# Six mix operations behind the scale, the low parts of the mixes on GpSimd, and two more hidden tiles split early

## The chip, the cores and the metric

The kernel runs on one NeuronCore of a Trainium2 chip. The metric is the device time of one execution in microseconds. Before the change it is 3221.83 us, the median of three runs (3221.02 to 3222.63). Five engines run queues of their own and wait for each other through semaphores: TensorE (PE) multiplies, VectorE (DVE) and ScalarE (ACT) work element by element, GpSimd (POOL) does the same more slowly, and SyncE (SP) issues the loads of weights.

## The reference

Two blocks stand one behind the other over 512 positions of width 1024, all in float32. The first has two kinds of attention, a cross attention and a gated MLP; the second has two layers. Each of these two layers holds two SwiGLU feed-forwards, four in all, and the change is in these:

```python
def swiglu(x, w13, w2):
    gate, up = jnp.split(x @ w13, 2, axis=-1)
    return (jax.nn.silu(gate) * up) @ w2

h = h + 0.5 * rms_norm_2(swiglu(rms_norm_2(h, g[0]), ffn_w13[i, 0], ffn_w2[i, 0]), g[1])
```

The inner width is 2816, that is 22 tiles of 128.

## The kernel before

A float32 value is multiplied as a high part and a low part. ACT makes the high part (a cast, `split_hi`, L329 for weights), DVE subtracts it from the value to make the low part (`split_lo`, L345), and PE does three products: high by high, low by high, high by low (L528). Weights come in chunks of 128 x 2048 float32 (1 MB), in two slots.

Each feed-forward has three stretches. The texts call the four feed-forwards FF1 to FF4; they start their mixes at about 903, 1554, 1978 and 2810 us.

1. The first four units of the up projection (gate and value of one hidden tile each), in `linear` with `paired="filled"`. The norm is deferred: PE multiplies the unscaled tiles first (units 0 and 1 together, then 2, then 3), while ACT squares the tiles, DVE adds the squares (L869), PE sums them over partitions (L812), DVE makes the mean (L878), ACT the root (L786), DVE the reciprocal (L880) and a diagonal matrix (L882), and PE spreads the scale over all partitions with two matmuls (L853), 5/16 through the first half of unit 2. `keep_scale` copies it for later use (L1149). Unit 2 takes the high weights first, its low weights (the first L345 shown below) last. Unit 3 waits for both parts of its weights at its start: the second L345. The results are scaled on DVE (L2456), pass the Silu on ACT (L2451) and are multiplied on DVE (L2459).
2. The other eighteen hidden tiles, in `sevenths`: seven products in the place of eight quarter products, Strassen's way. These need, next to the inputs, four mixes of quarters of the normed input. The `Mixing` class makes them in four steps j = 0 to 3, each with four DVE operations of 128 x 256 (L2533, L2535, L2538, L2541), whose inputs are both in SBUF. ACT makes the high part of a step (`mix_high`, L2546, 128 x 1024), which waits for all four operations of that step; DVE makes its low part (`mix_low`, L2550). PE needs all four low parts for the product S1 of the first of the eighteen.
3. The down projection (`linear` over 22 hidden tiles in halves of 11). `HiddenHalves` splits the hidden tiles: the high parts (L2584) on ACT, the low parts (L2588) on DVE. The first `EARLY` of them are split between the last operations of `sevenths`, ahead of the last Silu (L2771), the rest after it. PE takes weights of 128 x 1408 here.

The order on each engine is the order of the code; nothing reorders it. POOL has, in the norms of FF2 to FF4, seven additions of 128 x 512 to `h` (L931), which come ahead of all this and end before the squares are made. SP issues the load of chunk n+2 when the low part of chunk n is made.

Of the kernel before, what the change touches and what calls it, by code (L numbers as in the profile page):

```python
# [28 lines left out]
KQ = KD // 2  # L29
# [16 lines left out]
F32 = mybir.dt.float32  # L46
# [187 lines left out]
def _build(nc, io, ctx, block):  # L234
# [14 lines left out]
    vec = place("vec", [P, NVEC])  # L249
# [370 lines left out]
    class Stage:  # L620
# [33 lines left out]
        def pool(self, pool):  # L654
            pass
# [57 lines left out]
    def vcol(name, k):  # L713
# [3 lines left out]
    n_square, n_add, n_sum, n_mean, n_root, n_scale, n_spread, n_value, n_onto, n_high, n_low = roles(  # L717
        "norm_squares_and_gains", "norm_adds", "norm_sums", "norm_means", "norm_roots", "norm_scales", "norm_spread", "norm_values_and_mixes", "norm_onto",
        "norm_highs", "norm_lows")
# [277 lines left out]
    class Deferred(Stage):  # L997

        scaled_late = True
        ahead = None  # L1000
# [1169 lines left out]
    mix = area("mix", [P, KD, T], 64 * KB)  # L2170
# [29 lines left out]
    def _(pe):  # L2200
# [4 lines left out]
           between={0: (lambda act: open_gates(act, 4, 2 * KD), None)})  # L2205
# [34 lines left out]
    def x_scale_act(act):  # L2240
# [6 lines left out]
           between={0: (x_scale_act, x_scale_dve)})  # L2247
# [174 lines left out]
    def tile_added(engine, t):  # L2422
# [4 lines left out]
           between={3: (conv_norm.early_act, conv_norm.early_dve)}, **summing(h, 2, onto=True, parted=False))  # L2427
# [19 lines left out]
    def swiglu(norm, meanwhile):  # L2447

        def act_part(act, k, products, u):
            act.wait_ge(dve_steps.sem, dve_steps.after(k, 1))  # L2450
            nc.scalar.activation(tmp[:, u, :], tmp[:, u, :], ACT.Silu).then_inc(act_steps.sem, 1)  # L2451

        def dve_part(dve, k, products, u):
            if k == 0:
                norm.wait_scale(dve)
            nc.vector.tensor_tensor(tmp[:, u, :], products[0], kept, ALU.mult).then_inc(dve_steps.sem, 1)  # L2456
            meanwhile[k](dve)
            dve.wait_ge(act_steps.sem, act_steps.after(k, 1))
            nc.vector.tensor_tensor(hid[:, k, :], products[1], tmp[:, u, :], ALU.mult).then_inc(psum_read.sem, 1)  # L2459

        return dict(act_part=act_part, dve_part=dve_part, steps=(1, 1))
# [36 lines left out]
    def conv_act(act, k, products, u):  # L2498
        for side in range(2):
# [8 lines left out]
           between={KF - 1: (split_second_down, None)})  # L2508
# [5 lines left out]
    mix_h, mix_l = area("mix_h", [P, 4, KQ, TH], 12 * KB, F32R), area("mix_l", [P, 4, KQ, TH], 28 * KB, F32R)  # L2514
    mix = area("mix", [P, KQ, 4, TH], 72 * KB)
    gained_2 = area("gained_second", [P, KQ, TH], 68 * KB)
    sum_2 = area("weight_sum_2", [P, QUARTER], 88 * KB)
    EARLY = 6
    FIRST, SECOND = slice(0, TH), slice(TH, T)
    w_sums, w_high, w_low, w_made, w_kept, w_gate, w_value = sb_cut, sb_soft_h, sb_soft_l, sb_z, sb_zc, sb_open, sb_keep  # L2520

    class Mixing(Deferred):
# [4 lines left out]
            nc.scalar.activation(gained_2[:, j, :], h[:, j, SECOND], ACT.Copy,  # L2527
                                 scale=vec[:, self.gain + j:self.gain + j + 1]).then_inc(n_square.sem, 1)

        def mixed(self, dve, j):  # L2530
            g1, g2 = (vec[:, self.gain + t:self.gain + t + 1] for t in (j, KQ + j))
            dve.wait_ge(n_square.sem, n_square.after(j, 1))
            nc.vector.scalar_tensor_tensor(mix[:, j, 0, :], h[:, j, FIRST], g1, gained_2[:, j, :], ALU.mult,  # L2533
                                           ALU.subtract).then_inc(n_value.sem, 1)
            nc.vector.scalar_tensor_tensor(mix[:, j, 1, :], h[:, KQ + j, SECOND], g2, gained_2[:, j, :], ALU.mult,  # L2535
                                           ALU.subtract).then_inc(n_value.sem, 1)
            dve.wait_ge(n_value.sem, n_value.after(j, 1))
            nc.vector.scalar_tensor_tensor(mix[:, j, 2, :], h[:, KQ + j, SECOND], g2, mix[:, j, 0, :], ALU.mult,  # L2538
                                           ALU.add).then_inc(n_value.sem, 1)
            dve.wait_ge(n_value.sem, n_value.after(j, 3))  # L2540
            nc.vector.scalar_tensor_tensor(mix[:, j, 3, :], h[:, KQ + j, FIRST], g2, mix[:, j, 2, :], ALU.mult,  # L2541
                                           ALU.subtract).then_inc(n_value.sem, 1)
# [2 lines left out]
            act.wait_ge(n_value.sem, n_value.after(j, 4))  # L2545
            nc.scalar.copy(mix_h[:, :, j, :], mix[:, j, :, :]).then_inc(n_high.sem, 1)  # L2546

        def mix_low(self, dve, j):
            dve.wait_ge(n_high.sem, n_high.after(j, 1))
            nc.vector.tensor_tensor(mix_l[:, :, j, :], mix[:, j, :, :], mix_h[:, :, j, :].bitcast(F32),  # L2550
                                    ALU.subtract).then_inc(n_low.sem, 1)

        def squares_act(self, act):
# [3 lines left out]

        def squares_dve(self, dve):
            Deferred.squares_dve(self, dve)
            for j in range(KQ):  # L2560
                self.mixed(dve, j)

        def scale_act(self, act):
            self.mix_high(act, 0)
            self.mix_high(act, 1)
            self.two.square_root(act)
            nc.scalar.activation(spare[:, 0:1], spare[:, 1:2], ACT.Silu)
            self.mix_high(act, 2)
            self.mix_high(act, 3)
            self.keep_scale(act)  # L2570

    class HiddenHalves(Stage):
# [35 lines left out]
    def sevenths(name, norm, base, halves_, down):  # L2608
# [134 lines left out]
        def emit():  # L2743
# [10 lines left out]
            @block.scalar  # L2754
            def _(act):
                def seed(u):
                    wait_used(act, u, "A11")
                    evicted_before(act, u)
                    nc.scalar.copy(bank_b(u), bank_a(u)).then_inc(w_kept.sem, 1)

                def keep_five(u):
                    wait_used(act, u, "S1")
                    nc.scalar.copy(five(u), bank_e(u)).then_inc(w_kept.sem, 1)

                def keep_u2(u):
                    wait_used(act, u, "S2")
                    nc.scalar.copy(gate_of(u, SECOND), bank_b(u)).then_inc(w_kept.sem, 1)

                def silu(u):
                    act.wait_ge(w_gate.sem, w_gate.after(u, SCALED))  # L2770
                    nc.scalar.activation(gate_of(u, EVERY), gate_of(u, EVERY), ACT.Silu).then_inc(w_kept.sem, 1)  # L2771

                for u in range(count):
                    high(act, u, "S3")
                    if u:
                        silu(u - 1)
                    if u < last:
                        high(act, u + 1, "A11")
                    else:
                        halves_.high(act, 0)  # L2780
                    seed(u)
                    if u < last:
                        high(act, u + 1, "S1")
                    else:
                        halves_.high(act, 1)
                    keep_five(u)
                    high(act, u, "A22")
                    if u < last:
                        high(act, u + 1, "S2")
                    else:  # L2790
                        halves_.high(act, 2)
                        halves_.high(act, 3)
                    keep_u2(u)
                    if u < last:
                        high(act, u + 1, "A12")
                        high(act, u + 1, "S4")
                    else:
                        halves_.high(act, 4)
                        wait_used(act, last, "A12")
                        split_hi(act, down, 16 * (down // 2 + 1), down % 2, order[down][2])  # L2800
                        halves_.high(act, 5)
                silu(last)

            @block.vector
            def _(dve):
# [23 lines left out]
                def first_hidden(u):  # L2829
                    wait_used(dve, u, "A22")  # L2830
                    nc.vector.tensor_tensor(hid[:, WHOLE + u, FIRST], bank_b(u), gate_of(u, FIRST), ALU.mult).then_inc(psum_read.sem, 1)
# [36 lines left out]
                halves_.low(dve, 5)  # L2868
                second_hidden(last)
                first_hidden(last)  # L2870

            @block.tensor
            def _(pe):
# [56 lines left out]
    def feed_forward(layer, n, norm, after_up=None, sums=None):  # L2930

        up, down = f"up_{layer}{n}", first[f"down_{layer}{n}"]
        for s, per in ((n_square, 1), (n_value, 4), (n_high, 1), (n_low, 1)):
            s.stage(per, KQ)
        read, rest = psum_read.total, up + "_sevenths"
        halves_ = HiddenHalves(read, first[rest] + count_of[rest] + 2, down + 1)
        (first_act, first_dve), ahead, last_dve, emit = sevenths(rest, norm, read + WHOLE, halves_, down)

        def first_mix(dve):
            norm.mix_low(dve, 0)  # L2940

        def mixes(dve):
            norm.mix_low(dve, 1)
            norm.mix_low(dve, 2)

        def last_mix(dve):
            norm.mix_low(dve, 3)

        between = {0: (None, first_mix), 2: (first_act, None), 3: ahead}
        linear(up, KD, 256, x_split, norms=norm, between=between, paired="filled", quartered=True, next_ahead=False,  # L2950
               **swiglu(norm, (mixes, last_mix, first_dve, last_dve)))
        emit()
        linear(f"down_{layer}{n}", HALF, P, hid_split, halves=True, second_ahead=True, norms=halves_,
               between={3: after_up()} if after_up else {}, **(sums or summing(ybuf, 1, scale=kept)))
# [1774 lines left out]
```

## Time and profile before

| | |
|---|---|
| median of three runs | 3221.83 us |
| the profiled execution | 3223.61 us, with a span of 3221.8 us |
| TensorE busy | 3149.5 us of the span (98%) |
| VectorE, ScalarE, GpSimd busy | 2142.4, 1481.5, 136.4 us |
| mean granted TensorE clock | 0.996 |

The span is from the first to the last instruction of the trace. Every time inside it is counted from its start. An operation's record begins when it is handed to its unit and ends when its result is written, so that records of one engine overlap by some 0.1 us, and a record also holds the time in which the operation stands at a port. A wait is idle time of the engine ahead of an instruction, with the instruction that ended it.

### The profile page before, as it was taken

The page shows a single profiled execution, that of the slowest core. Times are in us where ns is not written, and L with a number is a line of the kernel's source. Part 1 is how long each engine was busy: PE and PEld are TensorE (multiplying, and loading weights), DVE is VectorE, ACT ScalarE, POOL GpSimd, SP SyncE. Part 2 cuts the span into 40 slices and gives each one's busy share as a digit, 9 for nine tenths or more (in the row PEclk, how much of TensorE's full clock was granted, in tenths as well). Part 3 has the DMA queues.
Part 4 walks back from the last instruction along what each step waited for, and adds up shares of the span by engine and source line. Part 5 has one row for each costly group of instructions (what it writes and reads, how often), then busy time and mean ns, then how long its engine had stood idle before and what let it go on. Part 6 is the DMA issues. An engine that isn't in the chain of part 4 may idle for free. (4 is left out here: it accounts for less than half of the span.)

```text
span 3221.8 us, 54209 instructions
## 1 busy us (share of the span) xinstructions
PE 3149.5 (98%) x22914; PEld 2705.9 (84%) x22914; DVE 2142.4 (66%) x3127; ACT 1481.5 (46%) x2289; POOL 136.4 (4%) x134
## 2 busy tenths in 40 slices
PE   9999999999999999999999999999999999999998
PEld 7887787888889988988899887998777777799986
DVE  6546766775399835363898458986666665789737
ACT  3357644443255623432455345554336564455524
POOL 2100000000000001000100011000120000100002
PEclk9999999999999999999999999999999999999999
DMA  5311232222323323223133321333222000123331
GB/s 184 113 53 66 92 105 92 89 95 94 102 79 105 102 99 116 95 74 105 66 105 104 108 97 66 106 105 99 85 80 102 16 4 16 66 100 107 103 104 66
DMA packets 47249, 287.17 MB, mean 89 GB/s; under 512 B 6416, under 2 KB 6688, under 8 KB 21408
## 3 DMA queue, kind: packets, MB, share of 16 engines
q1 hardware_dynamic: 44960, 279.51, 25.6%
q0 software_dynamic: 2048, 4.20, 0.4%
q8 instruction: 182, 2.98, 0.4%
q14 instruction: 59, 0.48, 0.1%
HBM read 277.39 MB, written 2.10 MB: 87 GB/s over the span
## 5 line engine op out<-in xcount | busy, mean ns | idle before, releaser
L345 DVE TENSOR_TENSOR wl<-raw,wh 128x2048 fp32r<-128x2048 f32 (+3 forms) x211 | 425.0, 2014 | 326.0 <-ACT wh L329 325.6
L528 PE MATMUL ps<-xh,wh 128*128 128x512 f32 (+1 forms) x1312 | 520.0, 397 | 15.0 <-DVE xl L3625 3.4
L528 PE MATMUL ps<-xl,wh 128*128 128x512 f32 (+1 forms) x1312 | 494.4, 392 | 3.3 <-POOL xl L3522 3.0
L329 ACT CAST wh<-raw 128x2048 fp32r<-128x2048 f32 (+2 forms) x208 | 348.5, 1676 | 277.7 <-PE ps L528 266.9
L528 PE MATMUL ps<-xh,wl 128*128 128x512 f32 (+1 forms) x1312 | 471.3, 392 | 0.3 <-DVE wl L345 0.3
L2693 ACT CAST wh<-raw 128x512 fp32r<-128x512 f32 x432 | 262.6, 619 | 244.0 <-DVE raw L2712 113.3
L528 PE MATMUL ps<-hid_h,wh 128*128 128x512 f32 x880 | 343.3, 390 | 2.7 <-DVE wl L345 2.7
L528 PE MATMUL ps<-hid_l,wh 128*128 128x512 f32 x880 | 342.5, 389 | 0.0
L528 PE MATMUL ps<-hid_h,wl 128*128 128x512 f32 x880 | 342.4, 389 | 0.0
L2704 DVE TENSOR_TENSOR wl<-raw,wh 128x512 fp32r<-128x512 f32 x432 | 297.3, 690 | 65.6 <-ACT wh L2693 64.5
L2883 PE MATMUL ps<-mix_h,wh 128*128 128x256 f32 x1152 | 327.1, 284 | 1.8 <-DVE tmp L2822 1.3
L2884 PE MATMUL ps<-mix_l,wh 128*128 128x256 f32 x1152 | 326.0, 283 | 0.0
L2885 PE MATMUL ps<-mix_h,wl 128*128 128x256 f32 x1152 | 325.9, 283 | 0.0
L528 PEld LDWEIGHTS ps<-xh,wh 128*128 128x128 f32 (+1 forms) x1312 | 246.8, 188 | 83.2 <-issue 23.4
L528 PEld LDWEIGHTS ps<-xl,wh 128*128 128x128 f32 (+1 forms) x1312 | 245.9, 188 | 60.7 <-POOL xl L3522 3.8
L528 PEld LDWEIGHTS ps<-xh,wl 128*128 128x128 f32 (+1 forms) x1312 | 245.0, 187 | 54.2 <-issue 1.0
L2885 PE MATMUL ps<-xh,wl 128*128 128x256 f32 x864 | 244.5, 283 | 0.0
L2884 PE MATMUL ps<-xl,wh 128*128 128x256 f32 x864 | 244.5, 283 | 0.0
L2883 PE MATMUL ps<-xh,wh 128*128 128x256 f32 x864 | 244.5, 283 | 0.0
L2883 PEld LDWEIGHTS ps<-mix_h,wh 128*128 128x128 f32 x1152 | 221.0, 192 | 3.6 <-DVE tmp L2822 2.3
L2884 PEld LDWEIGHTS ps<-mix_l,wh 128*128 128x128 f32 x1152 | 221.1, 192 | 0.0
L2885 PEld LDWEIGHTS ps<-mix_h,wl 128*128 128x128 f32 x1152 | 221.1, 192 | 0.0
(538 smaller groups left out, 5939.5 us busy)
## 6 DMA issues: line engine op xcount, KB each, us to landing
raw<-in_up SPq DMA_DIRECT2D x88, 1024.0 KB, 4.9
raw<-in_down SPq DMA_DIRECT2D x64, 704.0 KB, 4.0
raw<-in_up_c SPq DMA_DIRECT2D x22, 1024.0 KB, 4.9
raw<-in_down_c SPq DMA_DIRECT2D x16, 704.0 KB, 4.1
raw<-in_gates SPq DMA_DIRECT2D x8, 1024.0 KB, 5.0
raw<-in_gv SPq DMA_DIRECT2D x8, 1024.0 KB, 4.9
raw<-in_gu SPq DMA_DIRECT2D x8, 1024.0 KB, 5.0
raw<-in_gout SPq DMA_DIRECT2D x8, 1024.0 KB, 4.8
```

The source lines that it names most:

```text
L329: nc.scalar.copy(wh[:, slot, 0:w], raw[:, slot, 0:w]).then_inc(hi_ready, 1)
L345: nc.vector.tensor_tensor(wl[:, slot, 0:w], raw[:, slot, 0:w], wh[:, slot, 0:w].bitcast(F32), ALU.subtract).then_inc(lo_ready, 1)
L528: last = nc.tensor.matmul(out, stationary, moving, start=(fresh and q == 0), stop=(t == kt - 1 and half == per - 1 and q == 2), skip_group ...
L2693: split = nc.scalar.copy(part(wh, u, what), source(u, what))
L2704: split = nc.vector.tensor_tensor(part(wl, u, what), source(u, what), part(wh, u, what).bitcast(F32), ALU.subtract)
L2883: nc.tensor.matmul(out, hi_w[:, at_], hi, start=(fresh and j == 0), stop=False, skip_group_check=True)
L2884: nc.tensor.matmul(out, hi_w[:, at_], lo, start=False, stop=False, skip_group_check=True)
L2885: done = nc.tensor.matmul(out, lo_w[:, at_], hi, start=False, stop=(j == KQ - 1), skip_group_check=True)
```

## The change

Three edits, in all four feed-forwards.

`EARLY` goes from 6 to 8: the high parts of hidden tiles 6 and 7 stand on ACT ahead of the last Silu, and the low parts on DVE stand behind the last product. `mixed` is cut in two, `mixed_first` (two operations) and `mixed_rest` (the other two). Ahead of the scale stand steps 0 and 1 and the first two operations of step 2; the rest of step 2 and the whole of step 3 stand behind the scale and the first L345. The high parts of steps 2 and 3 move on ACT behind the copy of the scale. The low parts of all four steps are subtracted on POOL.

```diff
-    EARLY = 6
+    EARLY = 8
-        def mixed(self, dve, j):
+        def mixed_first(self, dve, j):
...
+        def mixed_rest(self, dve, j):
+            g2 = vec[:, self.gain + KQ + j:self.gain + KQ + j + 1]
             dve.wait_ge(n_value.sem, n_value.after(j, 1))
...
-        def mix_low(self, dve, j):
-            dve.wait_ge(n_high.sem, n_high.after(j, 1))
-            nc.vector.tensor_tensor(mix_l[:, :, j, :], mix[:, j, :, :], mix_h[:, :, j, :].bitcast(F32),
+        def pool(self, pool):
+            Deferred.pool(self, pool)
+            for j in range(KQ):
+                self.mix_low(pool, j)
+
+        def mix_low(self, pool, j):
+            pool.wait_ge(n_high.sem, n_high.after(j, 1))
+            nc.gpsimd.tensor_tensor(mix_l[:, :, j, :], mix[:, j, :, :], mix_h[:, :, j, :].bitcast(F32),
...
-            for j in range(KQ):
-                self.mixed(dve, j)
+            for j in (0, 1):
+                self.mixed_first(dve, j)
+                self.mixed_rest(dve, j)
+            self.mixed_first(dve, 2)
...
-            self.mix_high(act, 2)
-            self.mix_high(act, 3)
             self.keep_scale(act)
...
-                        halves_.high(act, 5)
+                        for t in range(5, EARLY):
+                            halves_.high(act, t)
...
                 first_hidden(last)
+                for t in range(6, EARLY):
+                    halves_.low(dve, t)
...
+        def high_mixes(act):
+            norm.mix_high(act, 2)
+            norm.mix_high(act, 3)
+
         def first_mix(dve):
-            norm.mix_low(dve, 0)
...
+            norm.mixed_rest(dve, 2)
+            norm.mixed_first(dve, 3)
+            norm.mixed_rest(dve, 3)
...
-        between = {0: (None, first_mix), 2: (first_act, None), 3: ahead}
+        between = {0: (high_mixes, first_mix), 2: (first_act, None), 3: ahead}
...
-               **swiglu(norm, (mixes, last_mix, first_dve, last_dve)))
+               **swiglu(norm, (nothing, nothing, first_dve, last_dve)))
```

The queue of DVE around the scale, before, in FF1. L2538 and L2541 are the last two operations of step 3, L2550 the low parts of the mixes.

```order
L2538 SCALAR_TENSOR_TENSOR mix_7492<-h_53,vec_49,mix_7492 128x256
L2541 SCALAR_TENSOR_TENSOR mix_7492<-h_53,vec_49,mix_7492 128x256
L878 TENSOR_SCALAR stats_59<-ps 128x4
L880 RECIPROCAL stats_59<-stats_59 128x4
L882 TENSOR_TENSOR rs_56<-const_58,stats_59 128x512
L345 TENSOR_TENSOR wl_52<-raw_50,wh_51 128x2048
L2550 TENSOR_TENSOR mix_l_7491<-mix_7492,mix_h_7490 128x4x256
L2456 TENSOR_TENSOR tmp_57<-ps,tmp_57 128x512
L2550 TENSOR_TENSOR mix_l_7491<-mix_7492,mix_h_7490 128x4x256 x2
L2459 TENSOR_TENSOR hid_4768<-ps,tmp_57 128x512
L345 TENSOR_TENSOR wl_52<-raw_50,wh_51 128x2048
```

The same place after the change. L2541 and L2544 are now the third and the fourth operation of a step.

```order
L2533 SCALAR_TENSOR_TENSOR mix_7492<-h_53,vec_49,gained_second_7493 128x256
L2535 SCALAR_TENSOR_TENSOR mix_7492<-h_53,vec_49,gained_second_7493 128x256
L878 TENSOR_SCALAR stats_59<-ps 128x4
L880 RECIPROCAL stats_59<-stats_59 128x4
L882 TENSOR_TENSOR rs_56<-const_58,stats_59 128x512
L345 TENSOR_TENSOR wl_52<-raw_50,wh_51 128x2048
L2541 SCALAR_TENSOR_TENSOR mix_7492<-h_53,vec_49,mix_7492 128x256
L2544 SCALAR_TENSOR_TENSOR mix_7492<-h_53,vec_49,mix_7492 128x256
L2533 SCALAR_TENSOR_TENSOR mix_7492<-h_53,vec_49,gained_second_7493 128x256
L2535 SCALAR_TENSOR_TENSOR mix_7492<-h_53,vec_49,gained_second_7493 128x256
L2541 SCALAR_TENSOR_TENSOR mix_7492<-h_53,vec_49,mix_7492 128x256
L2544 SCALAR_TENSOR_TENSOR mix_7492<-h_53,vec_49,mix_7492 128x256
```

Six operations went behind L345, and the four low parts left the queue; L2456, L2459 and the second L345 follow the twelve rows directly. The queue of POOL holds them now: the first row is FF1's, the last FF2's.

```order
L2558 TENSOR_TENSOR mix_l_7491<-mix_7492,mix_h_7490 128x4x256 x4
L466 UNCONDITIONAL_BRANCH
L931 TENSOR_TENSOR h_53<-tmp_57,h_53 128x512 x7
L466 UNCONDITIONAL_BRANCH
L931 TENSOR_TENSOR h_53<-tmp_57,h_53 128x512 x7
L2558 TENSOR_TENSOR mix_l_7491<-mix_7492,mix_h_7490 128x4x256 x4
```

They stand behind all other POOL work of their stage. The queue of ACT at the end of the eighteen tiles, after the change; L2592 are the high parts of the hidden tiles (L2584 before), L2779 is the last Silu.

```order
L2775 COPY tmp_57<-ps 128x256
L2592 CAST hid_h_4766<-hid_4768 128x512
L329 CAST wh_51<-raw_50 128x1408
L2592 CAST hid_h_4766<-hid_4768 128x512 x3
L2779 ACTIVATE tmp_57<-tmp_57 128x512
L438 UNCONDITIONAL_BRANCH
L2592 CAST hid_h_4766<-hid_4768 128x512
L329 CAST wh_51<-raw_50 128x1408
```

Before, one high part stood there between L329 and the Silu, and three between the Silu and the next L329.

## Rows read from the trace of the kernel before

**Rows 1.** The page's first part: busy time and share of each engine.
```profile
PE 3149.5 (98%) x22914; PEld 2705.9 (84%) x22914; DVE 2142.4 (66%) x3127; ACT 1481.5 (46%) x2289; POOL 136.4 (4%) x134
```
**Rows 2.** PE's waits: engine, line, waited for: us in total, times, longest.
```profile
PE ps L853 <- DVE rs L882: 9.0, 3, 3.0
```
**Rows 3.** Timeline of PE: start, us, engine line; FF2, then FF1.
```profile
1559.68 0.39 PE L528 MATMUL ps<-xl,wh 128*128 128x512 f32 x1
1563.08 2.07 PE L853 MATMUL ps<-rs,const 128*128 128x512 f32 x2 [3.01 <-DVE rs L882]
...
912.46 1.02 PE L853 MATMUL ps<-rs,const 128*128 128x512 f32 x2
```
**Rows 4.** FF2's windows: us, busy PE, PEld, DVE, ACT, POOL, clock, DMA, GB/s.
```profile
1553.00:1575.00 22.00, 18.62 (x77) 14.16 (x76) 21.24 (x33) 13.85 (x19) 0.00 (x0) 0.92 0.27 87
...
1563.00:1565.00 2.00, 1.93 (x3) 0.89 (x4) 2.00 (x2) 1.99 (x4) 0.00 (x0) 0.50 0.00 0
```
**Rows 5.** Timeline of DVE in FF2.
```profile
1559.58 0.48 DVE L2541 SCALAR_TENSOR_TENSOR mix<-h,vec,mix 128x256 f32<-128x256 f32 x1
...
1561.29 0.48 DVE L2541 SCALAR_TENSOR_TENSOR mix<-h,vec,mix 128x256 f32<-128x256 f32 x1
...
1562.33 0.69 DVE L882 TENSOR_TENSOR rs<-const,stats 128x512 f32<-128x512 f32 x1
...
1565.14 1.22 DVE L2550 TENSOR_TENSOR mix_l<-mix,mix_h 128x1024 fp32r<-128x1024 f32 x1
...
1569.75 2.28 DVE L345 TENSOR_TENSOR wl<-raw,wh 128x2048 fp32r<-128x2048 f32 x1
...
1585.34 0.69 DVE L2456 TENSOR_TENSOR tmp<-ps,tmp 128x512 f32<-128x512 f32 x1 [4.44 <-PE ps L528]
```
**Rows 6.** Timeline of ACT in FF2.
```profile
1557.31 2.13 ACT L2546 CAST mix_h<-mix 128x1024 fp32r<-128x1024 f32 x2
...
1567.59 1.90 ACT L329 CAST wh<-raw 128x2048 fp32r<-128x2048 f32 x1
```
**Rows 7.** Timelines of DVE and POOL ahead of FF2, where both work; and one POOL line.
```profile
1536.44 1.34 DVE L1110 SCALAR_TENSOR_TENSOR xl<-h,vec,xh 128x512 fp32r<-128x512 f32 x1
...
1546.60 0.75 DVE L1110 SCALAR_TENSOR_TENSOR xl<-h,vec,xh 128x512 fp32r<-128x512 f32 x1 [0.31 <-ACT xh L1057]
...
1535.94 1.30 POOL L931 TENSOR_TENSOR h<-tmp,h 128x512 f32<-128x512 f32 x1 [1.29 <-DVE tmp L924]
...
L931 POOL TENSOR_TENSOR h<-tmp,h x42: 1277/1740/1756, 1242.8 to 3163.2; 128x512 f32<-128x512 f32 x42
```
**Rows 8.** Timelines of FF1: ACT, PE, DVE.
```profile
907.23 1.99 ACT L2546 CAST mix_h<-mix 128x1024 fp32r<-128x1024 f32 x2
...
908.34 0.95 PE L812 MATMUL ps<-const,rs 128*128 128x1 f32 x8
...
918.78 2.28 DVE L345 TENSOR_TENSOR wl<-raw,wh 128x2048 fp32r<-128x2048 f32 x1
```
**Rows 9.** The first matmul of unit 3, in FF1 and FF2.
```profile
921.98 0.39 PE L528 MATMUL ps<-xh,wh 128*128 128x512 f32 x1
...
1574.26 0.39 PE L528 MATMUL ps<-xh,wh 128*128 128x512 f32 x1
```
**Rows 10.** A long split on DVE beside POOL, in the layer behind FF3.
```profile
2345.39 3.12 DVE L345 TENSOR_TENSOR wl<-raw,wh 128x2048 fp32r<-128x2048 f32 x1
...
2344.88 1.48 POOL L3575 TENSOR_TENSOR dx<-hn 128x511 f32<-128x511 f32 x1
```
**Rows 11.** The start of the down product of FF2: DVE, ACT, PE.
```profile
1772.77 0.69 DVE L2588 TENSOR_TENSOR hid_l<-hid,hid_h 128x512 fp32r<-128x512 f32 x1 [0.78 <-ACT hid_h L2584]
1782.79 1.62 DVE L345 TENSOR_TENSOR wl<-raw,wh 128x1408 fp32r<-128x1408 f32 x1
...
1768.75 0.63 ACT L2771 ACTIVATE tmp<-tmp 128x512 f32<-128x512 f32 x1 [2.33 <-DVE tmp L2817]
...
1784.56 0.47 PE L528 MATMUL ps<-hid_h,wh 128*128 128x512 f32 x1 [0.42 <-DVE wl L345]
```

More of the change, by code:

```diff
@@ L2937, in feed_forward, with nothing @@
         (first_act, first_dve), ahead, last_dve, emit = sevenths(rest, norm, read + WHOLE, halves_, down)
+        def high_mixes(act):
+            norm.mix_high(act, 2)
+            norm.mix_high(act, 3)
         def first_mix(dve):
-            norm.mix_low(dve, 0)
[L2942 to L2947, printed above, removed]
-        between = {0: (None, first_mix), 2: (first_act, None), 3: ahead}
+            norm.mixed_rest(dve, 2)
+            norm.mixed_first(dve, 3)
+            norm.mixed_rest(dve, 3)
+        def nothing(dve):
+            pass
+        between = {0: (high_mixes, first_mix), 2: (first_act, None), 3: ahead}
         linear(up, KD, 256, x_split, norms=norm, between=between, paired="filled", quartered=True, next_ahead=False,
-               **swiglu(norm, (mixes, last_mix, first_dve, last_dve)))
+               **swiglu(norm, (nothing, nothing, first_dve, last_dve)))
         emit()
```

## The prediction

> **What bounds the kernel now.** I read the busy times first: TensorE (PE) is busy 3149.5 of 3221.8 us [rows 1], so a change is worth what it takes from, or adds to, PE's idle time and the time at the lower clock. Next PE's waits over the whole program, longest in total first [rows 2]: the longest is the wait of the spread matmuls at L853 for the vector engine's (DVE's) L882, 9.0 us in three waits of 3.0 us. The four feed-forward stages (FF1 to FF4, starting their mixes at about 903, 1554, 1978 and 2810 us) hold them: FF2, FF3 and FF4 one L853 wait each, FF1 none. Then the timelines around these places.
>
> In FF2 the last PE work ahead of the spread starts at 1559.68 and ends near 1560.07; the spread starts at 1563.08 [rows 3]. DVE runs sixteen mix operations without a break up to L2541 at 1561.29, and only then L878, L880 and L882, which starts at 1562.33 [rows 5]. The granted clock is 0.50, the 1.2 GHz level, from 1563 to 1565 us, after a wait of 3.0 us, and 0.92 in the mean over 22 us [rows 4]: the fall costs 0.08 x 22 = 1.7 us (1.65 to 1.87 by the rounding). So each of three stages has 3.0 + 1.7 = 4.7 us to give.
>
> **The six mix operations behind the scale.** One mix step has a cadence of 1561.29 - 1559.58 = 1.71 us for four operations [rows 5]. Ten stand ahead of L878 now, sixteen before: the six are 0.51 + 0.40 (rest of step 2) and 1.71 (step 3), 2.62 us. Alone this moves L882 and the spread 2.62 us forward, leaves a wait of 0.4 us, and with no wait near 3 us the clock fall should go too: 4.28 us of PE's time in each of FF2 to FF4. It does not all arrive. Unit 3, whose first matmul is at 1574.26 [rows 9], waits for the low parts of its weights, the second L345 at 1569.75, which ends at 1572.03 and stands in DVE's queue behind the six. With L345 after L882, the six, the scaling L2456, ScalarE's (ACT's) two high parts of 1.04 us each, its Silu (0.60), L2459, and ACT's L329 (1.8) ahead of it [rows 5, 6], undisturbed it would end at about 1570.85. So the move alone is worth 1574.26 - 1570.9 = 3.4 us in each of three stages; in FF1, where the spread at 912.46 doesn't wait [rows 3], that L345 ends at 921.06 and unit 3 starts at 921.98 [rows 8, 9], it is worth nothing.
>
> **The low parts on GpSimd (POOL).** Sixteen subtractions of 128x1024 leave DVE, 1.22 us each [rows 5]. POOL's two-input operation of 128x512 takes 1.28 to 1.30 us undisturbed [rows 7]. No row shows 128x1024 there: it is over 1.28 us and not over twice that, 2.56. I take 2.35, near the upper end, because DVE's own subtraction nearly doubles with the width (L882, 512 columns, 0.69 us; L2550, 1024, 1.22, [rows 5]), and POOL's should by more, its part per element being larger. The Trainium skill (GPSIMD Engine Reference, 3.1 Elementwise) has 4.50 us for a two-input add of 2048 elements; half of it is 2.25, which would take 0.1 us from each POOL operation and under 1.5 us from the sum below.
>
> Now what DVE does meanwhile. L1110 reads two tiles of SBUF. Undisturbed it takes 0.75 us; at 1536.44, with a POOL operation running from 1535.94 to 1537.24, it takes 1.34 and ends at 1537.78, 0.54 behind POOL's end [rows 7]. L345 takes 2.28 us, but 3.12 at 2345.39, and ends 2.15 us behind the POOL operation that ended at 2346.36 [rows 10]. POOL's L931 likewise has a median of 1.740 us against a smallest of 1.277 [rows 7]. The two don't overlap: one stands while the other runs. L2456 reads one input from PSUM, and I take it as outside this queue. Every mix operation, L882 and L345 read two SBUF tiles, so they all queue with POOL's 2.35 us.
>
> Step by step in FF2 (estimates from these rows: after a DVE operation POOL ends 2.22 us later; after POOL a 256-column operation ends 0.27 us later, L882 0.54, L345 2.15). ACT's first high part ends at 1558.35 [rows 6], POOL asks at 1558.42 while DVE is in its ninth operation, gets the ports at its end (1558.75) and ends at 1560.97. The tenth ends at 1561.24; L882, which starts 0.56 us behind the last mix operation's end (1562.33 - 1561.77), is ready at 1561.8, but the second POOL operation has been waiting since 1561.0 and runs to 1563.46: L882 ends at 1564.0 instead of 1563.02. The spread is 0.95 us **later** than now, and the clock fall stays. L345 ends at 1566.15, step 2 is complete at 1567.0; its high part ends at 1568.1, POOL asks at 1568.2, 0.1 us ahead of the last mix operation, and runs to 1570.45; that operation ends at 1570.7. Then ACT's high part (1571.8), Silu (1572.4), L329 (1574.2), and L345 from 1574.3 to 1576.55. Unit 3 starts at 1576.6 instead of 1574.26: +2.35 us. FF3 and FF4 have the same order and the same distances: 3 x 2.35 = +7.05 us. In unit 3 DVE has 4.44 us of idle time ahead of 1585.34 [rows 5], so the rest of its queue is absorbed.
>
> FF1: the first high part ends at 908.27, the sums at 909.29 [rows 8]; POOL runs 908.35 to 910.7 and holds L882 to 911.25, still ahead of the spread at 912.46. The second POOL operation goes ahead of L345, which ends at 915.6, step 2 is complete at 916.5, and by the same steps the mixes are complete at 920.2 and the second L345 at 926.0, against 921.06 now. Unit 3 waits from 921.98 to 926.05: +4.1 us, and a wait of over 3 us brought the lower clock in all three places where it stood: +1.7. FF1 together +5.8.
>
> **The last product.** DVE's L345 at 1782.79 ends 0.42 us after PE wants it (the matmul at 1784.56), with 0.78 us of DVE idle at 1772.77, waiting for ACT's high part [rows 11]. ACT sits idle 2.33 us ahead of the Silu at 1768.75, which hides two high parts of 0.52 us; the two low parts keep their place in DVE's queue. The third L345 comes 0.8 us earlier and the wait goes: 0.46, 0.42, 0.45, 0.43 in the four stages, -1.8 us. If that cover failed (ACT's Silu late by 1 us) nothing on PE waits for it within 5 us.
>
> **Sum.** +5.8 + 7.05 - 1.8 = +11.1 us on the profiled execution of 3223.6 us, which lies 1.8 us above the median of the runs shown: 3232.9 us for the median.
> The two ends of that unknown duration: with POOL at 1.28 us the same walk gives +0.9 in FF1, -0.95 in each other stage (spread at 1561.9, wait of 1.9 us), together -3.8; at 2.56 about +13.5.
>
> **Rivals.**
> Alternation lost in one place: the last mix operation is 0.1 us behind POOL's third request, which is less than I can read. If DVE goes first there, the mixes are complete at 1568.7, L345 is held by POOL's fourth and ends at 1575.4: +1.15 in three stages, +2.85 in FF1 (a wait just under 3 us, clock open), -1.8: +4.5 to +6.2, say 3227.
> DVE goes first wherever its queue has no gap: L882 ends at 1561.9, POOL gets in only beside L2456, L345 ends at 1573.35: -0.9 three times, +0.6, -1.8: -3.9, 3218. No row shows POOL's request against two back-to-back SBUF operations of DVE. For it: L882 follows a gap of 0.27 us, which lets one POOL operation in and no more. Against: a median of L931 half a microsecond over its smallest says that POOL and DVE take turns where both are ready again and again. The Trainium skill (SBUF — State Buffer, Who interferes with whom) says that the order of issue decides which of the two is blocked, for the whole instruction. By that rule the request at 1561.0 comes ahead of L882's, and the walk above holds; the pairs in rows 7 and 10 agree with it.
> L882 early: as the walk, but it slips in before the second POOL operation; the spread is at 1562.0, the clock stays up, PE is 2.7 us early, and then waits 5 us for the same L345 with a fall there: +4 in three stages, +16, 3238.
> No contention (that side of the result: faster): -3.4 x 3 - 1.8 = -12, 3210. It decides if 128x1024 on POOL leaves DVE's durations as they are; all of rows 7 and 10 speak against it.
>
> **How the numbers follow.** The walk 0.40; lost alternation 0.20; DVE first 0.14; L882 early 0.12; no contention 0.14. What a measurement tells from no change is 0.2%, 6.4 us. Faster: no contention, 0.14. Same: lost alternation and DVE first, less 0.02 for stages in which the alternation is kept: 0.32. Slower: 0.40 + 0.12 + 0.02 = 0.54. The range of 8 in 10 leaves out the case of no contention below and a little above 16 us: 3217 to 3240.
>
> **What would show it.** Right: POOL at about 2.3 us for each low part; L882 or the tenth mix operation over 2 us long by the record; PE's wait for L882 still there at three places; a new wait of unit 3 for L345, longest in FF1 (4 us) with a clock of 0.50 behind it; the 0.4 us waits gone from the down products. Wrong: L882's wait gone from PE's list and the second L345 ending before unit 3 wants it, or DVE operations that keep 0.48 and 2.28 us beside POOL.

## The result and the profile after

| | median, us | runs | ratio to before | 95% interval |
|---|---|---|---|---|
| before, in the same session | 3221.77 | 5 | | |
| changed | 3235.45 | 5 | 1.0039 | 1.0028 to 1.0051 |
| changed, a second session (before: 3221.43) | 3232.76 | 5 | 1.0033 | 1.0021 to 1.0046 |

The change costs 13.7 us in one session and 11.3 in the other; 3232.9 was predicted. The profiled execution took 3236.69 us, its span is 3234.9. In the changed kernel the mix operations are L2533, L2535, L2541 and L2544, the low parts L2558 (on POOL), the high parts L2549, and the low parts of hidden tiles L2596.

Busy time, from the page of the changed kernel; it answers to [rows 1]:
```profile
PE 3153.2 (97%) x22914; PEld 2710.4 (84%) x22914; DVE 2147.2 (66%) x3111; ACT 1482.7 (46%) x2289; POOL 175.7 (5%) x150
```
POOL took over sixteen operations of 2.4 us, 39 us in all. DVE gave up sixteen of 1.22 us, 19.5 us, and yet is busy 4.8 us **longer**: its records now hold time in which an operation stands at a port. PE's waits of the changed kernel, longest in total first; they answer to [rows 2]:
```profile
PE ps L528 <- DVE wl L345: 14.0, 11, 4.2
PE ps L853 <- DVE rs L882: 12.0, 3, 4.0
```
The wait for the scale grew from 9.0 to 12.0 us in the same three places; that for the low parts of weights has a longest of 4.2 us. PE's timeline of the changed kernel at the spread of the scale in FF2, at the start of unit 3 in FF2 and in FF1, and at the second unit of FF2's down product; it answers to [rows 3, 9, 11]:
```profile
1569.91 2.08 PE L853 MATMUL ps<-rs,const 128*128 128x512 f32 x2 [3.99 <-DVE rs L882]
...
1582.71 0.47 PE L528 MATMUL ps<-xh,wh 128*128 128x512 f32 x1 [1.63 <-DVE wl L345]
...
926.36 0.77 PE L528 MATMUL ps<-xh,wh 128*128 128x512 f32 x1 [4.18 <-DVE wl L345]
...
1791.63 0.47 PE L528 MATMUL ps<-hid_h,wh 128*128 128x512 f32 x1
```
The last row has no bracket: the 0.42 us of the down product is gone. POOL and DVE of the changed kernel in FF2; DVE's rows answer to [rows 5]:
```profile
1564.27 5.04 POOL L2558 TENSOR_TENSOR mix_l<-mix,mix_h 128x1024 fp32r<-128x1024 f32 x2 [12.69 <-ACT mix_h L2549]
1574.14 2.39 POOL L2558 TENSOR_TENSOR mix_l<-mix,mix_h 128x1024 fp32r<-128x1024 f32 x1 [4.83 <-ACT mix_h L2549]
1577.98 2.41 POOL L2558 TENSOR_TENSOR mix_l<-mix,mix_h 128x1024 fp32r<-128x1024 f32 x1 [1.45 <-ACT mix_h L2549]
```
```profile
1564.51 2.60 DVE L2535 SCALAR_TENSOR_TENSOR mix<-h,vec,gained_second 128x256 f32<-128x256 f32 x1
...
1567.66 2.19 DVE L882 TENSOR_TENSOR rs<-const,stats 128x512 f32<-128x512 f32 x1
1569.78 2.28 DVE L345 TENSOR_TENSOR wl<-raw,wh 128x2048 fp32r<-128x2048 f32 x1
...
1574.19 2.62 DVE L2544 SCALAR_TENSOR_TENSOR mix<-h,vec,mix 128x256 f32<-128x256 f32 x1
...
1578.46 0.69 DVE L2459 TENSOR_TENSOR hid<-ps,tmp 128x512 f32<-128x512 f32 x1 [1.05 <-ACT tmp L2451]
...
1580.27 2.29 DVE L345 TENSOR_TENSOR wl<-raw,wh 128x2048 fp32r<-128x2048 f32 x1 [1.11 <-ACT wh L329]
```
Read the two together. The two low parts run from 1564.27 to 1569.31. The tenth mix operation (0.48 us undisturbed) takes 2.60 and L882 (0.69) takes 2.19, each ending shortly behind a POOL operation. At 1574.14 POOL asks 0.05 us ahead of L2544 and wins; that one takes 2.62. L2459, with one input in PSUM, keeps 0.69 us while POOL's fourth operation (1577.98 to 1580.39) is running. In FF1, DVE's timeline of the changed kernel:
```profile
911.26 4.47 DVE L345 TENSOR_TENSOR wl<-raw,wh 128x2048 fp32r<-128x2048 f32 x1
...
917.87 2.62 DVE L2544 SCALAR_TENSOR_TENSOR mix<-h,vec,mix 128x256 f32<-128x256 f32 x1
...
923.92 2.29 DVE L345 TENSOR_TENSOR wl<-raw,wh 128x2048 fp32r<-128x2048 f32 x1 [1.10 <-ACT wh L329]
```
There the first L345 meets the second low part, and unit 3's L345 ends at 926.21, 5.15 us later than before. Windows of the changed kernel (columns as in [rows 4]):
```profile
1553.00:1575.00 22.00, 17.63 (x73) 13.34 (x72) 20.93 (x29) 12.79 (x19) 5.90 (x3) 0.92 0.22 73
...
924.00:931.00 7.00, 4.64 (x11) 3.70 (x12) 6.24 (x8) 2.02 (x4) 0.02 (x1) 0.52 0.44 150
```
FF2 has its clock fall as before. FF1, which had none, now runs at 0.52 for 7 us around its new wait.

**Where the time went.** Both kernels have the same matmuls in the same order, so the n-th one of after less the n-th of before (each from its span's start) shows how the delay grows: 0 at FF1's mixes, +6.7 behind unit 3 of FF1; +5.8 at FF2's mixes, +8.4 at its unit 3; +7.1 and +9.9 in FF3; +11.3 and +13.9 in FF4; +13.1 at the end. The stages cost 6.7, 2.6, 2.8 and 2.5 us, 14.6 in all. Between them 3.7 us come back, nearly all of it 0.9 us in each down product, 3.5 in all; a wait of before (0.50 us at 1609.62) also did not recur. Between FF3 and FF4 2.2 us are lost net, 2.9 of them in two clock falls in code that the change doesn't touch.

### The profile page after: what moved, and what is told of

It is laid out like the page before. It is cut to its first block and busy times, and to the rows that moved or that the text cites. A ratio compares the mean times of both kernels' runs of the same rounds, so it can differ in the third digit from the quotient of the medians.

```text
span 3234.9 us, 54209 instructions
## 1 busy us (share of the span) xinstructions
PE 3153.2 (97%) x22914; PEld 2710.4 (84%) x22914; DVE 2147.2 (66%) x3111; ACT 1482.7 (46%) x2289; POOL 175.7 (5%) x150
## 5 line engine op out<-in xcount | busy, mean ns | idle before, releaser
L345 DVE TENSOR_TENSOR wl<-raw,wh 128x2048 fp32r<-128x2048 f32 (+3 forms) x211 | 427.2, 2025 | 329.2 <-ACT wh L329 328.8
L329 ACT CAST wh<-raw 128x2048 fp32r<-128x2048 f32 (+2 forms) x208 | 348.6, 1676 | 277.5 <-PE ps L528 266.5
```

The lines of the kernel that those rows point to most:

```text
L329: nc.scalar.copy(wh[:, slot, 0:w], raw[:, slot, 0:w]).then_inc(hi_ready, 1)
L345: nc.vector.tensor_tensor(wl[:, slot, 0:w], raw[:, slot, 0:w], wh[:, slot, 0:w].bitcast(F32), ALU.subtract).then_inc(lo_ready, 1)
```

## Experiments

The first four ran in one session (before: 3222.99 us, 21 runs), the others in a second (before: 3221.43, 9 runs). Theory: GpSimd's operation and DVE's operations with two SBUF inputs exclude each other for a whole instruction, and these turns delay the scale and the second L345. Rivals: the new order alone costs the time (the second L345 stands behind six mix operations and two high parts); or `EARLY` does.

### The same order, low parts on DVE

```diff
-            pool.wait_ge(n_high.sem, n_high.after(j, 1))
-            nc.gpsimd.tensor_tensor(mix_l[:, :, j, :], ...
+            dve.wait_ge(n_high.sem, n_high.after(j, 1))
+            nc.vector.tensor_tensor(mix_l[:, :, j, :], ...
...
-               **swiglu(norm, (nothing, nothing, first_dve, last_dve)))
+               **swiglu(norm, (early_lows, late_lows, first_dve, last_dve)))
```
`early_lows` makes the low parts of steps 0 and 1, `late_lows` those of 2 and 3.

> The changed kernel with the low parts of the mixes back on DVE: low parts 0 and 1 while ScalarE makes the first Silu, 2 and 3 behind the second L345. Nothing is left out of the computation. Port theory (POOL's subtraction and DVE's operations with two SBUF inputs exclude each other): PE's wait for L882 falls from 4.0 to 0.4 us in FF2 to FF4 and the lower clock with it, the second L345 ends near 2.6 to 3.4 us earlier than in the kernel before relative to the stage, so -3.4 us in each of three stages, 0 in FF1, about -2 for the early hidden tiles: 12 us faster than before, near 3210. Rival (the move of the six operations itself delays the second L345): as slow as the changed kernel, 8 to 13 us slower than before.

Measured: 3211.07 us, ratio 0.9965 (0.9951 to 0.9978), 11.9 us below before. PE's timeline in FF2, then a window over FF1's unit 3:
```profile
1559.34 1.13 PE L853 MATMUL ps<-rs,const 128*128 128x512 f32 x2 [0.44 <-DVE rs L882]
1570.00 0.47 PE L528 MATMUL ps<-xh,wh 128*128 128x512 f32 x1 [0.90 <-DVE wl L345]
```
```profile
924.00:931.00 7.00, 7.00 (x33) 5.79 (x32) 6.44 (x11) 2.40 (x4) 0.00 (x0) 1.00 0.16 64
```
The scale's wait is 0.44 instead of 3.99 us, unit 3's 0.90 instead of 1.63, and the clock stays up. The order is a gain. The engine of sixteen instructions, with the places that they take in its queue, makes the difference between 11.9 us faster and the change's 11.3 to 13.7 slower. The rival of the order falls.

### EARLY alone

Before, with only the edit of `EARLY` and its two loops.

> The kernel before with EARLY at 8 instead of 6 and nothing else. The wait of 0.42 to 0.46 us for L345 at the second unit of each down product goes: -1.8 us at least, and up to -3 if the positions in the changed kernel's trace (0.6 to 0.8 us gained between the sevenths and the down product of each stage) come from this edit alone. Rival (those came from the later start of the stage): -0.5 or nothing.

Measured: 3218.26 us, ratio 0.9983 (0.9974 to 0.9992), that is -4.7 us (-8.4 to -2.6). Against the matmuls of before, each down product gains 0.9 us, 3.5 in all: more than the wait of 0.42 to 0.46 us that the edit was meant to remove, and more than the 1.8 to 3 expected. The interval holds this 3.5; that the rest of the 4.7 is an effect of the edit is not shown. In the profiled execution, which ends 5.6 us ahead of before's, 1.4 us come from FF3, which has the same wait for the scale (2.97 us) and no clock fall behind it. `EARLY` is not what costs. Windows of this kernel and of before:
```profile
1986.00:1990.00 4.00, 4.00 (x19) 3.29 (x18) 4.00 (x5) 2.91 (x4) 0.00 (x0) 1.00 0.73 254
```
```profile
1986.00:1990.00 4.00, 3.34 (x7) 2.03 (x8) 4.00 (x4) 3.54 (x5) 0.00 (x0) 0.57 0.18 27
```

### Low parts on POOL, nothing else

Before, with `mix_low` on POOL and no mix operation moved (the POOL lines of the change's diff alone).

> The kernel before with the low parts of the mixes on POOL and nothing else: all sixteen mix operations stand ahead of the scale. Port theory: two POOL operations of 2.4 us each go in between the mix operations, L882 comes 4 us later, PE waits 7 us for it in FF2 to FF4 (+4 each) and, in FF1, 3.5 us where it did not wait, with a lower clock behind it (+5): 17 us slower than before. Rival (POOL costs nothing here, the six moved operations do the damage): 0 to +1 us.

Measured: 3242.02 us, ratio 1.0064 (1.0048 to 1.0079), +19 us. DVE in FF2, then PE at L853 in FF1 and FF2:
```profile
1562.71 2.60 DVE L2535 SCALAR_TENSOR_TENSOR mix<-h,vec,gained_second 128x256 f32<-128x256 f32 x1
1565.23 2.56 DVE L2538 SCALAR_TENSOR_TENSOR mix<-h,vec,mix 128x256 f32<-128x256 f32 x1
...
1570.57 0.69 DVE L882 TENSOR_TENSOR rs<-const,stats 128x512 f32<-128x512 f32 x1
```
```profile
916.47 1.12 PE L853 MATMUL ps<-rs,const 128*128 128x512 f32 x2 [3.59 <-DVE rs L882]
...
1571.32 2.08 PE L853 MATMUL ps<-rs,const 128*128 128x512 f32 x2 [7.23 <-DVE rs L882]
```
With sixteen mix operations ahead of the scale both turns fall on 256-column operations, and L882 keeps its 0.69 us but comes 4.2 us late. So each of the two POOL operations costs DVE's queue some 2.1 us here too; the longer DVE queue only moves the place. In one point the expectation failed: FF1's wait of 3.59 us brought no lower clock (granted clock 1.00 from 912 to 930 us).

### POOL behind the second L345

```diff
             Deferred.pool(self, pool)
+            pool.wait_ge(lo_ready, self.ahead + 3)
             for j in range(KQ):
```


> The changed kernel with one wait more on POOL: its four subtractions start when the second L345 is done. Same instructions on the same engines, at another time. Port theory: L882 and both L345 are undisturbed, so the four front stretches go as without POOL (-3.4 us in each of three stages against before); POOL then works beside DVE's splits in unit 3, which has 4.4 us of slack, and the first product S1 may wait 0 to 1.5 us in each stage: 6 to 12 us faster than before. Rival (what costs is the late completion of steps 2 and 3 and their high parts): as slow as the changed kernel.

Measured: 3227.49 us, ratio 1.0017 (1.0008 to 1.0026): +4.5 us where -6 to -12 was expected, a miss. The front of the stage did what was expected (0.48 at L853, 0.88 at unit 3 in FF2). The loss is a new wait. POOL, DVE, ACT and PE of this kernel in FF2:
```profile
1572.70 10.38 POOL L2559 TENSOR_TENSOR mix_l<-mix,mix_h 128x1024 fp32r<-128x1024 f32 x4 [25.38 <-DVE wl L345]
```
```profile
1574.59 0.68 DVE L2456 TENSOR_TENSOR tmp<-ps,tmp 128x512 f32<-128x512 f32 x1
1575.19 2.83 DVE L2713 TENSOR_TENSOR wl<-raw,wh 128x512 fp32r<-128x512 f32 x1
1577.94 2.88 DVE L2720 TENSOR_TENSOR raw<-raw 128x512 f32<-128x512 f32 x1
1580.75 2.88 DVE L2721 TENSOR_TENSOR raw<-raw 128x512 f32<-128x512 f32 x1
...
1586.78 0.69 DVE L2729 TENSOR_TENSOR raw<-weight_sum,raw 128x512 f32<-128x512 f32 x1
```
```profile
1587.56 0.62 ACT L2702 CAST wh<-raw 128x512 fp32r<-128x512 f32 x1 [1.50 <-DVE raw L2729]
...
1589.72 0.36 ACT L2768 COPY ps<-ps 128x256 f32<-128x256 f32 x1
```
```profile
1590.14 0.39 PE L2895 MATMUL ps<-mix_h,wh 128*128 128x256 f32 x1 [2.70 <-ACT ps L2768]
```
POOL's first operation (1572.70 to 1575.11) costs DVE nothing: it meets only operations with an input in PSUM, among them L2456 with its 0.68 us. Beside the other three, three of DVE's weight operations take 2.8 to 2.9 us instead of 0.68. DVE's sum L2729 comes late, ACT's high part waits for it, the copy L2768 stands behind that in ACT's queue, and PE waits 2.7 to 3.0 us in each stage (11.1 in all, at a product of the eighteen tiles). I had counted DVE's 4.4 us of idle time in unit 3 as cover; the three turns take more, about 6.5 us. Not all of the loss can be read here: the profiled execution (3223.95 us) is the fastest of the ten, 3.5 us under their median, with a mean granted clock of 0.997 where the others have 0.992 to 0.996. The rest probably lies in more time at the lower clock, but no trace shows it.

### POOL behind the scale

```diff
             Deferred.pool(self, pool)
+            self.two.wait(pool, n_scale, 2)
             for j in range(KQ):
```


> The changed kernel with one wait more on POOL: its subtractions start when L882 is done. Port theory, in which the second L345 decides: PE's wait for L882 falls from 4.0 to about 0.4 us in FF2 to FF4, but POOL's four operations now all stand behind the first L345, the second L345 ends no earlier than in the changed kernel, and PE, which comes 4 us earlier, waits 5 to 7 us for it with a lower clock behind: no better than the changed kernel, 13 to 20 us slower than before. Rival, in which the held L882 is what costs: 4 us of PE's time come back in each of three stages: level with before.

Measured: 3244.65 us, ratio 1.0069 (1.0053 to 1.0085), +23 us. POOL, DVE and PE in FF2:
```profile
1566.97 6.90 POOL L2559 TENSOR_TENSOR mix_l<-mix,mix_h 128x1024 fp32r<-128x1024 f32 x2 [14.82 <-DVE rs L882]
```
```profile
1566.80 2.28 DVE L345 TENSOR_TENSOR wl<-raw,wh 128x2048 fp32r<-128x2048 f32 x1
1569.01 2.62 DVE L2541 SCALAR_TENSOR_TENSOR mix<-h,vec,mix 128x256 f32<-128x256 f32 x1
1571.66 2.50 DVE L2544 SCALAR_TENSOR_TENSOR mix<-h,vec,mix 128x256 f32<-128x256 f32 x1
```
```profile
1566.94 1.12 PE L853 MATMUL ps<-rs,const 128*128 128x512 f32 x2 [0.43 <-DVE rs L882]
1583.84 0.77 PE L528 MATMUL ps<-xh,wh 128*128 128x512 f32 x1 [7.13 <-DVE wl L345]
```
With the scale fully protected the kernel is slower still, and slower than the 13 to 20 us expected: the second L345 decides. Three turns stand ahead of it (L2541, L2544 and the last L2544, 6.3 us in all), and unit 3 of FF2 starts 0.6 us later in its stage than in the changed kernel. The rest is clock: PE now loses its time in one wait of 7.13 us, and from 1579.5 to 1589.5 the granted clock is 0.50, which costs 2.8 us more behind the start of unit 3, against 0.1 in the changed kernel. L345 was issued 0.17 us ahead of POOL here and runs undisturbed; POOL's first operation stands behind it, the next two of DVE stand behind POOL's.

### Half operations on POOL

Each 128 x 1024 is issued as two of 128 x 512.

> The changed kernel with each of POOL's subtractions of 128x1024 cut into two of 128x512. If POOL and DVE take turns operation by operation, each DVE operation is held 1.3 us at most instead of 2.4: L882 comes 2.1 us earlier than in the changed kernel and PE waits 1.8 us for it with the clock up, then 4 us for the second L345: between 8 and 14 us slower than before. If POOL kept the ports until its queue is empty, L882 and PE's wait would be as in the changed kernel (4.0 us).

Measured: 3239.03 us in one run, so only its trace is used. DVE, then PE, in FF2:
```profile
1562.38 1.52 DVE L2535 SCALAR_TENSOR_TENSOR mix<-h,vec,gained_second 128x256 f32<-128x256 f32 x1
...
1564.45 1.11 DVE L882 TENSOR_TENSOR rs<-const,stats 128x512 f32<-128x512 f32 x1
1565.49 3.35 DVE L345 TENSOR_TENSOR wl<-raw,wh 128x2048 fp32r<-128x2048 f32 x1
1568.76 1.52 DVE L2541 SCALAR_TENSOR_TENSOR mix<-h,vec,mix 128x256 f32<-128x256 f32 x1
```
```profile
1565.62 1.12 PE L853 MATMUL ps<-rs,const 128*128 128x512 f32 x2 [1.82 <-DVE rs L882]
1579.51 0.77 PE L528 MATMUL ps<-xh,wh 128*128 128x512 f32 x1 [4.13 <-DVE wl L345]
```
Half the length on POOL halves DVE's stalls or does better (1.04 us over 0.48, 0.42 over 0.69, 1.07 over 2.28), but four operations of DVE stand in turn instead of two. So neither engine keeps the ports over several instructions: they change hands operation by operation. PE's waits were expected at 1.8 and 4 us and are 1.82 and 4.13; the time lies above the 8 to 14 us expected. In FF2 unit 3 even starts 1.1 us sooner in its stage than in the changed kernel. What is saved is lost to the clock: behind the longer wait for L345 it is 0.50 from 1578.2 to 1584.8, which costs 2.6 us behind the start of unit 3, against 0.1.

### The changed kernel again

> The changed kernel once more. The lower clock in the layer behind FF3, at 2392 and 2743 us of its trace, stands where the kernel before has the same waits and the full clock. If the two belong to the change they are there again; if they hang on how the execution falls against the chip's measuring of activity, they come and go between executions, and with them 1 to 3 us: 11 to 15 us slower than before.

Measured: 3232.76 us, +11.3. The wait at L853 is 3.98 to 4.01 us again. What moved is the clock. A window and unit 3 of FF3 in this execution:
```profile
1993.20:2000.00 6.80, 5.92 (x12) 4.01 (x13) 6.73 (x8) 1.64 (x2) 1.98 (x2) 0.50 0.40 141
```
```profile
2006.84 0.47 PE L528 MATMUL ps<-xh,wh 128*128 128x512 f32 x1 [0.19 <-DVE wl L345]
```
PE ran at 1.2 GHz for 6.8 us behind the scale's wait, not 3.4, and so came to unit 3 when its weights were nearly ready: 0.19 us instead of 1.44. In FF3 and FF4 the fall is paid out of the next wait, and the stages cost about the same. The two falls behind FF3 are missing here. Windows of the first execution, then of this one, and PE's last wait ahead of that place (before, then changed, first execution):
```profile
2392.00:2395.50 3.50, 3.50 (x10) 2.71 (x10) 3.50 (x6) 2.21 (x4) 0.00 (x0) 0.52 0.31 131
```
```profile
2391.00:2396.00 5.00, 5.00 (x24) 4.14 (x23) 5.00 (x8) 3.66 (x5) 0.00 (x0) 1.00 0.25 107
```
```profile
2382.13 0.47 PE L528 MATMUL ps<-xh,wh 128*128 128x512 f32 x1 [1.89 <-DVE xl L3625]
```
```profile
2391.29 0.47 PE L528 MATMUL ps<-xh,wh 128*128 128x512 f32 x1 [1.89 <-DVE xl L3638]
```
The same wait of 1.89 us stands there in both kernels. It is followed by a fall in one execution of the changed kernel and in none of before or of this one. The other traces have the wait too, 1.87 to 1.89 us long, and five of the seven have the fall, among them two kernels with no subtraction on POOL (the first and the last experiment here). The second fall, at 2743, stands in the first execution alone. So these 2.9 us come and go from one execution to the next, and the first of the two falls is not tied to the change at all. They are most of the 3.2 us between the two profiled executions, which end 13.1 and 9.8 us behind before's. Whether they also make the 2.4 us between the two sessions' differences is not shown; the two intervals overlap.

### The six behind the first scaling, the high parts behind the weights

Before, with `EARLY` of 8 and `mixed` cut in two as in the change. The six mix operations stand between L2456 and L2459 of the first hidden tile, the high parts 2 and 3 on ACT behind L329 for unit 3, and all four low parts on DVE behind the second L345. The six are still ahead of the second L345, but L329, which it waits for, no longer stands behind them and their high parts.
```diff
+        def last_mixes(dve):
+            norm.mixed_rest(dve, 2)
+            norm.mixed_first(dve, 3)
+            norm.mixed_rest(dve, 3)
+        def lows(dve):
+            for j in range(KQ):
+                norm.mix_low(dve, j)
...
+        between = {1: (high_mixes, None), 2: (first_act, None), 3: ahead}
...
+               **swiglu(norm, (last_mixes, lows, first_dve, last_dve)))
```


> No POOL. The six mix operations behind the scale and behind the scaling L2456 of unit 0, ScalarE's high parts 2 and 3 behind its L329 for unit 3, DVE's four low parts behind the second L345. In the run with the low parts on DVE, PE still waited 0.9 us for the second L345 in FF2 to FF4. Port theory with the queues as walked: this wait goes too, the wait for L882 stays at 0.4 us: 4.3 us faster in each of three stages and 2.4 for the early hidden tiles, 15 us faster than before and 2 to 3 faster than that run. Rival (the four low parts in unit 3 delay DVE's splits for the first of the eighteen tiles): a new wait of 1 to 3 us there in each stage, about 8 us faster than before.

Measured: 3206.93 us, ratio 0.9952 (0.9938 to 0.9966): 14.5 us faster than before and 25.8 faster than the changed kernel in the same session. PE's only bracket at the spread in FF2, and DVE's second L345:
```profile
1559.50 1.12 PE L853 MATMUL ps<-rs,const 128*128 128x512 f32 x2 [0.43 <-DVE rs L882]
```
```profile
1565.38 2.28 DVE L345 TENSOR_TENSOR wl<-raw,wh 128x2048 fp32r<-128x2048 f32 x1
```
That L345 ends at 1567.66, 2.2 us ahead of its end in the trace of the first experiment; unit 3 waits for nothing. 15 us were expected.

## Why the prediction was right

**POOL's duration** (taken as 2.35, bounds 1.28 and 2.56): 2.39 us undisturbed. Near the upper bound, as argued from DVE's own growth with the width.

**DVE's operations with two SBUF inputs stand behind POOL's, operation by operation.** Shown by the removal (3211), by the move to POOL alone (3242) and by the halves. The rival without contention would have needed 0.48 and 0.69 us beside POOL; the tenth operation took 2.60 and L882 2.19. The Trainium skill (SBUF — State Buffer, Who interferes with whom) states that a DVE instruction with two SBUF inputs contends with a GpSimd one that reads SBUF, that one with at most one SBUF input, outside the 2-port modes, doesn't, that the shared ports are an exclusive lock, and that the order of issue decides who blocks. The traces agree on each: with POOL behind the scale, L345 ahead of POOL by 0.17 us kept 2.28, and POOL's operation took 4.37 of its pair's 6.90 us; in the changed kernel POOL ahead of L2544 by 0.05 us stretched it to 2.62; L2459 kept 0.69, and L2456, with POOL behind the second L345, 0.68.

**L882 0.95 us later** (a wait of about 3.95): 3.99, 3.98 and 3.99. The rivals in which DVE goes first or L882 slips in are refused here.

**The third request** was the one step too close to read: 0.1 us in the walk, 0.05 to 0.07 in the trace, POOL ahead in all four stages. The order of the engines was right with half the predicted margin, so it was luck as much as reading; the other way was priced at 3227.

**Unit 3 in FF2 to FF4** (+2.35 each, +7.05): +2.6, +2.8, +2.5, together 7.9.

**FF1** (+4.1 and +1.7 of clock): the wait is 4.18 us. The clock costs 2.5: I took the price of the falls in FF2, in which PE waits 3.0 us; here the clock fell while PE was still waiting and stayed at 0.52 over the window of 7 us. The term is mis-sized by 0.8 us. It also rests on a premise that the traces don't bear out, that a wait of over 3 us brings the lower clock: 3.59 us in FF1 of the kernel with only the low parts moved brought none, and 1.87 to 1.89 us behind FF3 brought it in six of ten traces.

**EARLY** (-1.8): the four waits are gone, and each down product gains 0.9 us, together -3.5. The term counted only the four waits and is mis-sized by 1.7 us; what the other 0.4 us per stage are is open.

**The sum** was +11.1. The measured terms, 6.7 and 7.9 less 3.5, give the same +11.1: what was too small in the stages (1.7 us) and what was too small in `EARLY` cancel, and that is luck. The traces give +13.1 and +9.8 between first and last matmul, the medians +13.7 and +11.3. What the prediction lacks against the first is the clock behind FF3 (2.9 us), which the second execution doesn't show. What remains open is why the same wait is followed by a fall in some executions only; no run here separates that.

## What to carry to other kernels

GpSimd was no spare engine for work with SBUF inputs while VectorE ran operations with two: each GpSimd instruction that met one was added to VectorE's queue at nearly its full, longer duration. Beside VectorE's idle time and its operations with an input in PSUM it cost nothing; a place for it has to be sought there. Before an operation is moved behind a critical one, list everything behind it in its queue and price the next deadline, here the second split of the weights; the best version kept the low parts on VectorE, moved the same six operations one place further and put what depends on them behind that deadline. When two engines take turns, write down both request times: where they lie closer than the reading error, price both outcomes.

## What the hardware did that I had not expected

- A POOL operation of 128 x 1024 costs DVE between 2.0 and 2.2 us whether it meets a 256-column operation (2.60 instead of 0.48), a 512-column one in mid-queue (2.83 instead of 0.68) or L345 (4.47 instead of 2.28). It costs less where DVE's operation asks later: 1.50 us at L882, 0.4 at the second L345 of the kernel with only the low parts moved (2.66 instead of 2.28).
- The same PE waits are followed by different falls of the clock from 2.4 to 1.2 GHz: behind the scale's wait of 3.98 us in FF3, 3.4 us at the lower clock in one execution of the changed kernel and 6.8 in another; behind the wait of 2.97 us in FF3, one in before and none with `EARLY` alone. Six of ten traces have a fall behind the same wait of 1.87 to 1.89 us in the layer behind FF3. Single executions of before lie between 3219.4 and 3227.4 us (21 runs), the fastest with a mean granted clock of 0.997 and the slowest with 0.995: by estimate 0.002 of the clock is some 6 us, about as much as one edit here is worth.
- A longer fall need not cost more: PE's next wait, for weights that come at a fixed time, became shorter by what the clock took (0.19 instead of 1.44 us in FF3). A fall behind the last wait of the front stretch is paid in full: 2.6 to 2.8 us in FF2 of the two kernels with a wait of 4.13 and 7.13 us for unit 3's weights.
